# Latent attention on raw latents, the factor per token applied with the takes, rotations between query and key slabs

## The chip, the cores and the metric

The kernel runs on one core of one Trainium2 chip. Its time is device microseconds of one execution. The time before is the median of three runs, 3774.57 us (3770.84 to 3775.61).

## The reference

Two transformer blocks follow each other, both at 512 tokens and width 1024, all in f32. The change touches one mixer of the first block: the latent attention of its second layer. Cut to that part:

```python
def _mla_mixer(u, positions, w_down, q_norm, kv_norm, w_uq, w_ukv, w_out):
    cq, ckv, k_rope = split(u @ w_down, [384, 640])            # 384 + 256 + 64 columns
    q = (_rmsnorm(cq, q_norm) @ w_uq).reshape(b, s, 8, 128 + 64)
    kv = (_rmsnorm(ckv, kv_norm) @ w_ukv).reshape(b, s, 8, 128 + 128)
    q_nope, q_rope = q[..., :128], _rope(q[..., 128:], ...)
    k_nope, v = kv[..., :128], kv[..., 128:]
    k_rope = _rope(k_rope, ...)
    return _mla_attention(q_nope, q_rope, k_nope, k_rope, v) @ w_out
# _rmsnorm(x, g) = x * rsqrt(mean(x * x over the row) + 1e-6) * g
```

The norm of a latent is a gain per column and a factor per token. The gain must come ahead of the projection; the factor is the same for all columns of a token and can be multiplied in before or behind it.

## The kernel before, in words

Activations lie feature by token: `big` has 32 chunks of 128 features by 512 tokens. Weights come in slabs through a ring of four (`ring`), loaded by SyncE in one fixed order (`ORDER`); a slab's load waits until the slab three places ahead has been used up (`lin_done`). A slab of a layer of kind "fm" gives 256 output features for all 512 tokens and fills one of two pairs of PSUM banks (`LP[0]`, `LP[1]`), which alternate by slab. Before TensorE writes a pair again, it waits on `lin_taken0` or `lin_taken1`: VectorE must have copied out the slab before the last. Kind "tm" gives 256 features with the tokens on the partitions. `XB` are four more banks for small products. All engines run one program each, written out in order by hand, and meet only at semaphores; nothing plans or reorders.

Layers marked as cut multiply in three passes with operands split into a high and a low part: ScalarE writes the high part of a slab (`w_hi`, line 1023 by `high`) and GpSimd the rest (`w_lo`, line 1388). The latent attention has these layers:

- `mlad`, 3 slabs, cut: the down projection. Chunks 0 to 2 of `big` (CQ) are the query latent, 3 and 4 (CKV) the key and value latent, 5 (KR) the shared rotary key.
- `mlaq`, 6 slabs, plain f32: queries; chunks 6 to 13 (QN) without, 14 to 17 (QR) with rotation. QR is made by slabs 4 and 5.
- `mlak`, 4 slabs: keys (KN). `mlav`, 4 slabs of kind "tm": values. `mlao`: the output projection behind the attention.

After `mlad` the program before does this (TensorE lines 779 to 787, ScalarE 1247 to 1250, VectorE 1978 to 1988). For each of the two latents ScalarE squares its chunks one by one (`rms`), TensorE sums them over features with a matrix of ones, 512 columns a chunk (`square_sum`), ScalarE takes the root of the 128x512 tile, VectorE its reciprocal (`root`, line 1588) and multiplies chunk by gain and factor (line 1982), in place. `latent_ready` must be 2, both latents done, before TensorE starts `mlaq`. VectorE copies each slab out with one TENSOR_SCALAR of 128x1024 (`plain` line 1745, `tokens` line 1753).

After `mlav` come five rotations (`rotate` on TensorE, `turn` on GpSimd and VectorE): TensorE multiplies a chunk by a rotation matrix, GpSimd multiplies the chunk by the cosines (line 1468), VectorE the rotated one by the sines and adds the two (lines 1761, 1763). Two buffers alternate, so a chunk's rotation waits for the one two ahead. `attention` then waits for all rotations and for all copies (`groups_taken`).

The attention goes over 8 heads by 4 blocks of 128 queries. Unit n: TensorE makes the scores of n (128 to 512 keys wide, lines 449), transposes the probabilities of n - 2 (line 632) and multiplies those of n - 3 with the values. VectorE adds the mask and takes the maximum (line 1786), ScalarE the exponentials (line 1023), VectorE the division (line 1800).

Line 449 is the one matmul helper of the kernel, line 1023 ScalarE's helper. Of an f32 matmul two instructions stand in the trace, so 128x512 by 128x128 is two rows of MATMUL.

Of the kernel before, what the change touches and what calls it, by code (L numbers as in the profile page):

```python
# [23 lines left out]
ALU = mybir.AluOpType  # L24
ACT = mybir.ActivationFunctionType
AX = mybir.AxisListType

P = 128
T = 512
NB = T // P  # L30
# [150 lines left out]
CQ, CKV, KR, QN, QR, KN, MV = 0, 3, 5, 6, 14, 18, 26  # L181
# [4 lines left out]
def build(nc, x, small, consts, consts2, pos, adab, w, out):  # L186
    with ExitStack() as ctx:
        sems = {}

        def s(name):  # L190
            if name not in sems:
                sems[name] = ctx.enter_context(nc.semaphore(name))
            return sems[name]
# [16 lines left out]
        big = sb("big", [P, 32, T])  # L210
        wk = sb("wk", [P, 6, T])
        tabs = sb("tabs", [P, 4, T])
# [13 lines left out]
        rt = sb("rt", [P, T])  # L226
        rstd = sb("rstd", [P, T])
# [46 lines left out]
        def gate_row(i):  # L274

            return big[0:4, (GI, GF, 27, 28, 29)[i], :]

        AD = tmp[:, :, :].rearrange("p a (b t) -> p (a b) t", t=T)
        OD = [tabs[:, 0:3, :].rearrange("p a b -> p (a b)").rearrange("p (j t) -> p j t", j=2),
              wk[:, 0:3, :].rearrange("p a b -> p (a b)").rearrange("p (j t) -> p j t", j=2)]  # L280

        def cc(name, a=0, n=None):
            t, (o, wd) = (cst, COFF[name]) if name in COFF else (cst2, COFF2[name])
            return t[:, o + a:o + (wd if n is None else a + n)]
# [25 lines left out]
        def sp_(name, a=0, n=1):  # L310
            return sm[:, SOFF[name][0] + a:SOFF[name][0] + a + n]

        def blk(b):
            return slice(b * P, (b + 1) * P)
# [130 lines left out]
        def _(pe):  # L445
            pl = Place(pe, s)

            def mm(o, lhsT, rhs, start=True, stop=True):
                return pe.matmul(o, lhsT=lhsT, rhs=rhs, start=start, stop=stop)  # L449
# [79 lines left out]
                pl.ada += n_ada  # L529
                pl.cut += n if cut else 0  # L530

            def square_sum(n, weights):

                if pl.norm:
                    pe.wait_ge(s("rt_ready"), pl.norm)
                for c in range(n):
                    pe.wait_ge(s("sq_ready"), pl.sq + c + 1)
                    mm(XB[0][:, :], weights, sq[:, c % 2, :], start=c == 0, stop=c == n - 1)\
                        .then_inc(s("sq_used"), 1)
                pl.sq += n  # L540
                pl.norm += 1

            def total_sum():

                if pl.norm:
# [52 lines left out]
            def rotate(chunks, weights):  # L598
                for i, c in enumerate(chunks):
                    if pl.rope + i >= 2:  # L600
                        pe.wait_ge(s("rope_done"), pl.rope + i - 1)
                    mm(XB[1 + (pl.rope + i) % 2][:, :], weights, big[:, c, :]).then_inc(s("rot_done"), 1)
                pl.rope += len(chunks)
# [173 lines left out]

            ffn("gu10", "dn10")
            src, fresh = norm(u_hi1)
            linear("mlad", "fm", src, fresh=fresh)  # L780
            square_sum(3, cc("ones"))
            square_sum(2, cc("ones"))
            pl.got("latent_ready", 2)
            linear("mlaq", "fm", lambda c: big[:, CQ + c, :])
            linear("mlak", "fm", lambda c: big[:, CKV + c, :])
            linear("mlav", "tm", lambda c: big[:, CKV + c, :])
            rotate([KR] + list(range(QR, QR + 4)), cc("rot64"))

            def mla_score(hh, _, qb, bank):
                W = (qb + 1) * P  # L790
# [228 lines left out]
        def _(act):  # L1019
            pl = Place(act, s)  # L1020

            def f(o, i, fn, **kw):
                return act.activation(o, i, fn, **kw)  # L1023

            def rms(srcs, size):

                for c, src in enumerate(srcs):
                    if pl.sq + c >= 2:
                        act.wait_ge(s("sq_used"), pl.sq + c - 1)
                    f(sq[:, c % 2, :], src, ACT.Square).then_inc(s("sq_ready"), 1)  # L1030
                pl.sq += len(srcs)
                act.wait_ge(s("sq_used"), pl.sq)
                if pl.norm:
                    act.wait_ge(s("rstd_ready"), pl.norm)
                f(rt[:, :], XB[0][:, :], ACT.Sqrt, scale=1.0 / size, bias=cc("eps")).then_inc(s("rt_ready"), 1)
                pl.norm += 1

            def high(q, it=0):

                slab, width = CUT_SLABS[q]  # L1040
# [6 lines left out]
            def layer(name, take=None, last=False, behind=None):  # L1047


                n = WIDTH[name][0]  # L1050

                def body(k, it):
                    if take:
                        take(k, it)
                    high(pl.cut + k + 2, it)
                    if behind:
                        behind(k)

                slab_loop(act, n - 2, body, peel=n if name in SLAB_ORDER else None)
                for k in (n - 2, n - 1):  # L1060
                    if take:
                        take(k, 0)
                    if not last:
                        high(pl.cut + k + 2)
                    if behind:
                        behind(k)
                pl.slab += n
                pl.group += n
                pl.cut += n
# [174 lines left out]
            hrms()  # L1244
            high(pl.cut + 1)
            high_input(u_hi1, (N_MOD + 3 * 1) * DC)
            layer("mlad", last=True)
            pl.groups_taken()
            rms([big[:, CQ + c, :] for c in range(3)], 384)
            rms([big[:, CKV + c, :] for c in range(2)], 256)  # L1250
            skip("mlaq")
            skip("mlak")
            skip("mlav")
# [270 lines left out]
        def _(dve):  # L1524
# [34 lines left out]
            def take(name, body):  # L1559

                n = WIDTH[name][0]
                n_ada = beside(pl, name)

                def one(k, it):
                    dve.wait_ge(s("lin_done"), at(pl.slab + k + 1, it, RING))
                    body(k, it, (pl.group + k) % 2)
                    if n_ada == n or k < n_ada:
                        ada_take(UP0 + pl.ada + k, it)
                        a = UP0 + 1 + pl.ada + k
                        if a < N_ADA or not isinstance(it, int):  # L1570
                            ada_acc_(a, it)

                slab_loop(dve, n, one, chains=[(link, DC - 1)] if n_ada == n else (),
                          peel=peeled(pl, name, n, n_ada))
                pl.slab += n
                pl.group += n
                pl.ada += n_ada

            def dyn(t, k, it, step, n):

                a = step * k
                return slice(a, a + n) if isinstance(it, int) else bass.ds(it * step * RING + a, n)

            def root():

                dve.wait_ge(s("rt_ready"), pl.norm + 1)
                pl.norm += 1
                dve.reciprocal(rstd[:, :], rt[:, :]).then_inc(s("rstd_ready"), 1)
                dve.wait_ge(s("rstd_ready"), pl.norm)

            def root_total():

# [150 lines left out]
            def plain(dst0):  # L1743
                def body(k, it, p):
                    ts(big[:, bass.ds(it * 2 * RING + 2 * k + dst0, 2) if not isinstance(it, int)
                           else slice(dst0 + 2 * k, dst0 + 2 * k + 2), :], LP[p][:, :, :],
                       1.0, None, ALU.mult)\
                        .then_inc(s(f"lin_taken{p}"), 1)
                return body

            def tokens(dsts):
                def body(k, it, p):
                    ts(dsts[k], LPF[p].rearrange("p (t c) -> p t c", c=256), 1.0, None, ALU.mult)\
                        .then_inc(s(f"lin_taken{p}"), 1)
                return body

            def turn(chunks, t, sines=wk, cosines=S):
                for i, c in enumerate(chunks):
                    k = pl.rope + i
                    dve.wait_ge(s("rot_done"), k + 1)  # L1760
                    link(tt(sines[:, k % 2, :], t, XB[1 + k % 2][:, :], ALU.mult))
                    dve.wait_ge(s("rope_cos"), k + 1)
                    tt(big[:, c, :], sines[:, k % 2, :], cosines[:, k % 2, :], ALU.add).then_inc(s("rope_done"), 1)
                pl.rope += len(chunks)
                dve.wait_ge(s("rope_done"), pl.rope)
# [209 lines left out]

            ffn(1, 0, "gu10", "dn10")
            mod_in(1, 1)
            take("mlad", plain(0))
            for c0, n, name in ((CQ, 3, "q_norm"), (CKV, 2, "kv_norm")):
                root()  # L1980
                for c in range(n):
                    ins = stt(big[:, c0 + c, :], big[:, c0 + c, :], sp_(name, c), rstd[:, :], ALU.mult, ALU.mult)
                ins.then_inc(s("latent_ready"), 1)
                pl.got("latent_ready")
            take("mlaq", plain(QN))
            take("mlak", plain(KN))
            take("mlav", tokens(mv))
            turn([KR] + list(range(QR, QR + 4)), tabs[:, 2, :])
            attention(MLA_H, 192.0 ** -0.5, P, chunked, 0)
            residual(1, 1, "mlao")  # L1990
            ffn(1, 2, "gu11", "dn11")
# [419 lines left out]
```

## Time and profile before

| | |
|---|---|
| median of the runs shown | 3774.57 us |
| profiled execution, its own time | 3773.32 us |
| its span, first to last instruction | 3771.5 us |
| TensorE busy, share of the span | 3607.9 us, 96% |
| VectorE, ScalarE, GpSimd busy | 37%, 26%, 40% |
| mean granted TensorE clock | 0.959 |
| latent attention, end of `mlad` to start of the attention | 1602.3 to 1691.3 us |
| its attention, up to the first matmul of `mlao` | 1691.3 to 1779.7 us |

Times of rows are microseconds from the start of the span. A busy TensorE can be a slow one: its granted clock is either full (1.00, 2.4 GHz) or half (0.50, 1.2 GHz), and a matmul at half level takes up to twice as long while the engine still counts as busy.

### The profile page before, as it was taken

What the parts mean: (1) busy time and instruction counts of PE and PEld (TensorE: products, weight loads), DVE (VectorE), ACT (ScalarE), POOL (GpSimd) and SP (SyncE); (2) the same over time, 40 slices, a digit from 0 to 9 for tenths busy, and PEclk for the clock granted to TensorE, in tenths of its full rate; (3) what the DMA queues carried; (4) which work ended last, traced back from release to release, by engine and by line L of the source; (5) the groups of instructions that cost most, each with busy time, mean ns of one, the idle gap of its engine ahead of it and who ended that gap; (6) DMA issues with size and microseconds to landing.
All of it is one profiled execution on the core that took longest, in us unless ns stands there. A gap on an engine that the chain in (4) does not pass through costs nothing.

```text
span 3771.5 us, 40976 instructions
## 1 busy us (share of the span) xinstructions
PE 3607.9 (96%) x16154; PEld 2739.8 (73%) x16154; DVE 1392.2 (37%) x2572; ACT 966.7 (26%) x1207; POOL 1490.5 (40%) x521
## 2 busy tenths in 40 slices
PE   8999999899999999989999989989999999799999
PEld 7878777468887888745588866843888868437887
DVE  4454277534243422234211135752201167632010
ACT  2222222422223222203222233331212233322221
POOL 3445451035445545400354554401546445014453
PEclk9999998999999999989999989979999999899999
DMA  6434221024343433220223221201222222002222
GB/s 248 186 134 176 98 78 57 1 101 176 131 178 127 177 131 121 76 94 1 76 85 103 89 82 67 79 1 45 78 101 94 85 78 79 12 34 78 99 91 78
DMA packets 53863, 360.57 MB, mean 96 GB/s; under 512 B 5969, under 2 KB 6353, under 8 KB 16593
## 3 DMA queue, kind: packets, MB, share of 16 engines
q1 hardware_dynamic: 53712, 358.53, 26.2%
q8 instruction: 99, 1.62, 0.2%
q14 instruction: 52, 0.42, 0.0%
HBM read 356.41 MB, written 2.10 MB: 95 GB/s over the span
## 4 chain that ended last, share of the span: by engine, by line
PE 90%; DVE 6%; ACT 1%; issue 1%; DMA 1%; POOL 1%; SPq 0%; DVEq 0%; ACTq 0%; POOLq 0%
PE LP L449 80%; PE XB L449 9%; DVE S L1786 1%; PE XB L632 1%; DMA big<-w_ada 1%; PE LP L748 1%; ACT E L1023 0%; DVE tmp L1908 0%; DVE st L1906 0%; ACT sq L1023 0%; POOL wk L1446 0%; DVE gain L1623 0%; DVE wk L1806 0%; POOL w_lo L1388 0%; DVE u L1602 0%
## 5 line engine op out<-in xcount | busy, mean ns | idle before, releaser
L1388 POOL TENSOR_TENSOR w_lo<-ring,w_hi 128x2048 fp32r<-128x2048 f32 (+1 forms) x263 | 1122.8, 4269 | 683.1 <-ACT w_hi L1023 682.3
L449 PE MATMUL LP<-u_hi,w_hi 128*128 128x512 f32 x2480 | 992.0, 400 | 21.2 <-ACT u_hi L1023 17.0
L449 PE MATMUL LP<-u_hi,w_lo 128*128 128x512 f32 x2480 | 979.4, 395 | 0.0
L449 PE MATMUL LP<-u_lo,w_hi 128*128 128x512 f32 x2480 | 937.0, 390 | 0.0
L449 PE MATMUL LP<-big_r,w_hi 128*128 128x512 f32 x2432 | 749.9, 389 | 1.1 <-POOL w_lo L1388 1.1
L1023 ACT ACTIVATE w_hi<-ring 128x2048 fp32r<-128x2048 f32 (+1 forms) x263 | 468.7, 1782 | 823.8 <-PE LP L449 734.0
L449 PEld LDWEIGHTS LP<-u_hi,w_hi 128*128 128x128 f32 x2480 | 474.9, 191 | 136.9 <-issue 39.1
L449 PEld LDWEIGHTS LP<-u_hi,w_lo 128*128 128x128 f32 x2480 | 474.6, 191 | 101.8
L449 PEld LDWEIGHTS LP<-u_lo,w_hi 128*128 128x128 f32 x2480 | 466.4, 188 | 95.2 <-issue 0.5
L449 PEld LDWEIGHTS LP<-big_r,w_hi 128*128 128x128 f32 x2432 | 455.8, 188 | 95.7 <-issue 1.2
L449 PE MATMUL LP<-big_r,w_lo 128*128 128x512 f32 x1216 | 473.2, 389 | 0.0
L1429 POOL TENSOR_TENSOR big_r<-tmp,big_r 128x512 f32 (+2 forms) x120 | 192.4, 1603 | 685.2 <-DVE big_r L1639 685.2
L1446 POOL TENSOR_TENSOR wk<-wk,sq 128x512 f32<-128x512 f32 x66 | 84.7, 1283 | 686.2 <-ACT sq L1023 683.1
L1023 ACT ACTIVATE tmp<-LP 128x512 f32<-128x512 f32 (+1 forms) x120 | 85.5, 712 | 959.7 <-PE LP L449 959.7
L1644 DVE TENSOR_TENSOR tmp<-tmp,LP 128x512 f32<-128x512 f32 x88 | 60.5, 687 | 635.7 <-ACT tmp L1023 620.3
L449 PEld LDWEIGHTS LP<-big_r,w_lo 128*128 128x128 f32 x1216 | 228.2, 188 | 47.6
L449 PE MATMUL LP<-u,ring 128*128 128x512 f32 x512 | 221.9, 594 | 4.2 <-DVE u L2217 2.6
L1545 DVE SCALAR_TENSOR_TENSOR XB<-ada_in,csil,XB 128x256 f32<-128x256 f32 x390 | 191.0, 490 | 13.7
L449 PEld LDWEIGHTS LP<-u,ring 128*128 128x128 f32 x512 | 96.6, 190 | 127.1 <-issue 120.8
L1714 DVE SCALAR_TENSOR_TENSOR h<-LP,gate,h 128x512 f32 (+1 forms) x64 | 48.1, 751 | 356.9 <-PE LP L449 356.4
L1023 ACT ACTIVATE E<-S,stat 128x128 f32<-128x128 f32 (+3 forms) x160 | 89.2, 558 | 265.5 <-DVE stat L1789 188.6
L449 PE MATMUL XB<-big 64*128 64x128 f32 (+5 forms) x472 | 132.1, 515 | 17.2 <-DVE stat L1789 6.1
(260 smaller groups left out, 3193.2 us busy)
## 6 DMA issues: line engine op xcount, KB each, us to landing
ada_in<-w_ada SPq DMA_DIRECT2D x66, 1024.0 KB, 4.9
ring<-w_in SPq DMA_DIRECT2D x22, 1024.0 KB, 4.8
ring<-w_gu00a SPq DMA_DIRECT2D x11, 1024.0 KB, 7.1
ring<-w_gu00b SPq DMA_DIRECT2D x11, 1024.0 KB, 6.7
ring<-w_gu01a SPq DMA_DIRECT2D x11, 1024.0 KB, 6.8
ring<-w_gu01b SPq DMA_DIRECT2D x11, 1024.0 KB, 6.7
ring<-w_gu10a SPq DMA_DIRECT2D x11, 1024.0 KB, 6.7
ring<-w_gu10b SPq DMA_DIRECT2D x11, 1024.0 KB, 6.8
```

The costliest lines, as they stand in the source:

```text
L449: return pe.matmul(o, lhsT=lhsT, rhs=rhs, start=start, stop=stop)
L632: last = pe.transpose(XB[2 + k % 2][:, blk(b)], src[:, blk(b)], cc("ident"))
L748: last = pe.transpose(LP[1][:, j, blk(b)], E[:, 2 * (k % 2) + j, blk(b)], cc("ident"))
L1023: return act.activation(o, i, fn, **kw)
L1388: gp.tensor_tensor(w_lo[:, slab % RING, 0:width], ring[:, slab % RING, 0:width], w_hi[:, q % 2, 0:width].bitcast(F32), ALU.subtract).then_ ...
L1429: gp.tensor_tensor(big_r[:, lo, :], src, big_r[:, hi, :].bitcast(F32), ALU.subtract)\
L1446: gp.tensor_tensor(sqa, sqa, sq[:, c % 2, :], ALU.add).then_inc(s("sq_added"), 1)
L1545: ins = stt(part if c < DC - 1 else ada_acc[:, :], wv[:, c * 256:(c + 1) * 256], csil[:, c:c + 1], part, ALU.mult, ALU.add)
L1644: tt(o, tmp[:, p, 0:T].unsqueeze(1), LP[p][:, 1:2, :], ALU.mult))
L1714: stt(o, LP[p][:, 0:1, :], g, o, ALU.mult, ALU.add).then_inc(s(f"lin_taken{p}"), 1)
L1786: link(dve.tensor_tensor_reduce(out=S[:, k % 2, 0:W], in0=XB[k % 2][:, 0:W], in1=mask(qb, W), scale=1.0, scalar=LOWEST, op0=ALU.add, op1=A ...
```

## The change

`square_sum`, `rms` and `root` go. In their place:

- VectorE takes a slab of `mlad` as two TENSOR_SCALARs of 128x512, each times its gain (`latents`). So `big` holds latents with gain and without the factor per token. Ahead of it ScalarE squares the slab straight from PSUM (`latent_square`); VectorE waits for that.
- The sums over features are made with the tokens on the partitions: the squares are the weights and a single column of ones is moved (`latent_sums`), 12 products for the first latent and 8 for the second. Root and reciprocal are of 128x4. `latent_spread` turns such a column back into a row for all partitions: four products of 128 columns.
- TensorE starts `mlaq` right behind the sums of the first latent. Spread, the second latent's sums, and the rotation of KR stand behind the first three slabs of `mlaq`; the rotations of QR stand behind the first two slabs of `mlak`.
- VectorE copies a slab of `mlaq` or `mlak` out with one TENSOR_TENSOR, times the spread factor; for `mlav` the factor is per partition and block, read with a stride of zero.
- Behind `mlav` nothing is left; the attention waits for the last copy.

```diff
+        RQ, RKV = tabs[:, 0, :], tabs[:, 1, :]
+        def latent_root(i, b=0, n=NB):
+            return st[:, 16 + 4 * i + b:16 + 4 * i + b + n]
+        def latent_squares(c):
+            return Z[:, c, :] if c < 4 else tmpf[:, 1024:1536]
...
-            linear("mlad", "fm", src, fresh=fresh)
-            square_sum(3, cc("ones"))
-            square_sum(2, cc("ones"))
-            pl.got("latent_ready", 2)
-            linear("mlaq", "fm", lambda c: big[:, CQ + c, :])
-            linear("mlak", "fm", lambda c: big[:, CKV + c, :])
+            def latent_sums(i, chunks):
+                pe.wait_ge(s("latent_squared"), i + 2)
+                if i:
+                    pe.wait_ge(s("latent_root"), 1)
+                for c in chunks:
+                    for b in range(NB):
+                        last = mm(XB[3][:, 4 * i + b:4 * i + b + 1], latent_squares(c)[:, blk(b)], cc("ones", 0, 1),
+                                  start=c == chunks[0] and b == 0, stop=c == chunks[-1] and b == NB - 1)
+                last.then_inc(s("latent_summed"), 1)
+            def latent_spread(i):
+                pe.wait_ge(s("latent_recip"), i + 1)
+                if i:
+                    pe.wait_ge(s("latent_copied"), 1)
+                for b in range(NB):
+                    last = mm(XB[0][:, blk(b)], latent_root(i, b, 1).to_broadcast([P, P]), cc("ident"))
+                last.then_inc(s("latent_spread"), 1)
+            def behind_queries(k):
+                if k == 0:
+                    latent_spread(0)
+                    latent_sums(1, range(CKV, CKV + 2))
+                if k == 1:
+                    slab_taken(2)
+                    rotate((KR,), cc("rot64"))
+                if k == 2:
+                    latent_spread(1)
+            def behind_keys(k):
+                if k < 2:
+                    slab_taken(3 + 4 + k)
+                    rotate((QR + 2 * k, QR + 2 * k + 1), cc("rot64"))
+            linear("mlad", "fm", src, fresh=fresh, after=lambda k: latent_sums(0, range(CQ, CQ + 3)) if k == 2 else None)
+            slab_taken(1)
+            linear("mlaq", "fm", lambda c: big[:, CQ + c, :], after=behind_queries)
+            linear("mlak", "fm", lambda c: big[:, CKV + c, :], after=behind_keys)
             linear("mlav", "tm", lambda c: big[:, CKV + c, :])
-            rotate([KR] + list(range(QR, QR + 4)), cc("rot64"))
...
-            rms([big[:, CQ + c, :] for c in range(3)], 384)
-            rms([big[:, CKV + c, :] for c in range(2)], 256)
+            def latent_square(k, it):
+                act.wait_ge(s("lin_done"), pl.slab + k + 1)
...
+                f(o, LP[(first + k) % 2][:, 0:n, :], ACT.Square).then_inc(s("latent_squared"), 1)
+            layer("mlad", latent_square, last=True)
+            for i, size in enumerate((384, 256)):
+                pl.got("latent_summed")
+                f(latent_root(i), XB[3][:, 4 * i:4 * i + NB], ACT.Sqrt, scale=1.0 / size, bias=cc("eps"))\
+                    .then_inc(s("latent_root"), 1)
...
+            def latents(k, it, p):
+                pl.got("latent_squared")
...
+                    ins = ts(big[:, c, :], LP[p][:, i, :], g, None, ALU.mult)
+                ins.then_inc(s(f"lin_taken{p}"), 1)
...
+            def scaled(dst0, tile):
+                def body(k, it, p):
+                    tt(big[:, dst0 + 2 * k:dst0 + 2 * k + 2, :], LP[p][:, :, :],
+                       tile.unsqueeze(1).to_broadcast([P, 2, T]), ALU.mult).then_inc(s(f"lin_taken{p}"), 1)
+                return body
+            def queries_taken(k, it, p):
+                if k == 0:
+                    latent_recip(0)
+                    latent_copy(0, RQ)
+                queries(k, it, p)
+                if k == 0:
+                    latent_recip(1)
+                if k == 1:
+                    turn((KR,), tabs[:, 2, :])
+                if k == 2:
+                    latent_copy(1, RKV)
+            def keys_taken(k, it, p):
+                keys(k, it, p)
+                if k < 2:
+                    turn((QR + 2 * k, QR + 2 * k + 1), tabs[:, 2, :])
```

## Rows read from the trace of the kernel before

**Rows 1.** Chain of waits, 1560 to 1720: start, us, what it went through.
```profile
1567.10 35.16 PE LP L449 x144
...
1608.01 3.36 DVE rstd L1588
...
1618.37 61.05 PE LP L449 x168
1679.41 0.87 PE XB L449 x2
...
1691.33 6.94 PE XB L449 x12
```

**Rows 2.** Busy time by stretch: us, PE, PEld, DVE, ACT, POOL (instructions), clock, DMA, GB/s.
```profile
1560.00:1562.00 2.00, 1.14 (x9) 1.05 (x9) 2.00 (x2) 0.63 (x1) 2.00 (x1) 0.91 0.64 197
1602.00:1612.00 10.00, 5.14 (x12) 1.65 (x10) 5.18 (x3) 4.04 (x7) 0.00 (x0) 1.00 0.13 39
1618.00:1624.00 6.00, 5.63 (x8) 2.57 (x9) 0.31 (x1) 0.00 (x0) 0.00 (x0) 0.58 0.00 0
1679.00:1684.00 5.00, 2.62 (x7) 1.07 (x7) 4.03 (x4) 0.00 (x0) 2.48 (x2) 1.00 0.92 350
1685.00:1711.00 26.00, 23.64 (x51) 11.59 (x52) 9.56 (x34) 5.00 (x16) 3.58 (x3) 0.50 0.07 28
1712.00:1772.00 60.00, 57.80 (x288) 34.61 (x288) 31.29 (x132) 23.16 (x73) 0.00 (x0) 1.00 0.00 1
505.00:560.00 55.00, 55.00 (x228) 40.31 (x227) 44.04 (x51) 11.54 (x14) 28.68 (x11) 1.00 0.22 77
```

**Rows 3.** Timeline, norm ahead of `mlad`: start, us, engine, instruction, [idle before <- releaser].
```profile
1560.97 1.27 PE L449 MATMUL XB<-cst,sq 128*128 128x1 f32 x8 [0.86 <-ACT sq L1023]
...
1563.10 0.18 DVE L1595 RECIPROCAL st<-st 128x4 f32<-128x4 f32 x1
...
1563.34 2.08 PE L449 MATMUL XB<-cst,st 128*128 128x128 f32 x8 [1.09 <-DVE st L1595]
```

**Rows 4.** Groups by line, whole span: count, busy us, mean ns, idle before.
```profile
L1023 ACT ACTIVATE big<-LP 128x1024 f32<-128x1024 f32 x8 | 8.2, 1028 | 39.4 <-PE LP L449 39.4
L2229 DVE TENSOR_TENSOR tmp<-tmp,LP 128x1024 f32<-128x1024 f32 x32 | 39.1, 1221 | 281.1 <-ACT tmp L1023 281.1
```

**Rows 5.** Timeline, slabs of `mlad`, then single products around the two stalls.
```profile
1582.57 4.59 POOL L1388 TENSOR_TENSOR w_lo<-ring,w_hi 128x2048 fp32r<-128x2048 f32 x1 [13.61 <-ACT w_hi L1023]
...
1591.40 1.22 DVE L1745 TENSOR_SCALAR big<-LP 128x1024 f32<-128x1024 f32 x1 [9.66 <-PE LP L449]
...
1604.31 2.94 PE L449 MATMUL XB<-sq,cst 128*128 128x512 f32 x6 [2.07 <-ACT sq L1023]
...
1683.51 1.12 PE L449 MATMUL XB<-big,cst 128*128 128x512 f32 x2 [2.38 <-DVE big L1763]
```

**Rows 6.** Groups by line, 1575 to 1700.
```profile
L1468 POOL TENSOR_TENSOR S<-big,tabs 128x512 f32<-128x512 f32 x5 | 6.3, 1264 | 96.9 <-PE XB L449 94.3 <-DVE big L1763 2.7
...
L1761 DVE TENSOR_TENSOR wk<-tabs,XB 128x512 f32<-128x512 f32 x5 | 3.4, 679 | 0.1
```

**Rows 7.** Timeline of the attention, its first and its last heads.
```profile
1698.47 3.92 PE L449 MATMUL XB<-big 128*128 128x512 f32 x4
...
1713.71 2.08 PE L449 MATMUL XB<-big 128*128 128x512 f32 x4
...
1761.03 0.33 PE L632 MATMUL XB<-cst,E 128*128 128x128 f32 x1
...
1764.60 0.80 PE L449 MATMUL XB<-big 128*128 128x128 f32 x4
...
1766.81 1.22 PE L449 MATMUL XB<-big 128*128 128x256 f32 x4
...
1769.13 1.65 PE L449 MATMUL XB<-big 128*128 128x384 f32 x4
...
1771.77 2.08 PE L449 MATMUL XB<-big 128*128 128x512 f32 x4
```

More of the change, by code:

```diff
@@ L530, in linear @@
                 pl.cut += n if cut else 0
[L532 to L541, printed above, removed]
             def total_sum():
@@ L779, in _, with slab_taken @@
             src, fresh = norm(u_hi1)
-            linear("mlad", "fm", src, fresh=fresh)
-            square_sum(3, cc("ones"))
-            square_sum(2, cc("ones"))
-            pl.got("latent_ready", 2)
-            linear("mlaq", "fm", lambda c: big[:, CQ + c, :])
-            linear("mlak", "fm", lambda c: big[:, CKV + c, :])
+            first = pl.group
+            def slab_taken(k):
+                g = first + k
+                pe.wait_ge(s(f"lin_taken{g % 2}"), g // 2 + 1)
+            def latent_sums(i, chunks):
[31 more added lines that the diff above has]
+            linear("mlak", "fm", lambda c: big[:, CKV + c, :], after=behind_keys)
             linear("mlav", "tm", lambda c: big[:, CKV + c, :])
-            rotate([KR] + list(range(QR, QR + 4)), cc("rot64"))
             def mla_score(hh, _, qb, bank):
@@ L1023, in f @@
                 return act.activation(o, i, fn, **kw)
[L1025 to L1036, printed above, removed]
             def high(q, it=0):
@@ L1246, in _ @@
             high_input(u_hi1, (N_MOD + 3 * 1) * DC)
-            layer("mlad", last=True)
-            pl.groups_taken()
-            rms([big[:, CQ + c, :] for c in range(3)], 384)
-            rms([big[:, CKV + c, :] for c in range(2)], 256)
+            first = pl.group
+            def latent_square(k, it):
+                act.wait_ge(s("lin_done"), pl.slab + k + 1)
+                if k < 2:
+                    o, n = Z[:, 2 * k:2 * k + 2, :], 2
+                else:
+                    o, n = latent_squares(4).unsqueeze(1), 1
+                f(o, LP[(first + k) % 2][:, 0:n, :], ACT.Square).then_inc(s("latent_squared"), 1)
[4 more added lines that the diff above has]
+                    .then_inc(s("latent_root"), 1)
             skip("mlaq")
@@ L1582, in dyn @@
                 return slice(a, a + n) if isinstance(it, int) else bass.ds(it * step * RING + a, n)
[L1584 to L1589, printed above, removed]
             def root_total():
@@ L1977, in _ @@
             mod_in(1, 1)
[L1978 to L1987, printed above, removed]
@@ L1988, in _ @@
-            turn([KR] + list(range(QR, QR + 4)), tabs[:, 2, :])
+            def latents(k, it, p):
+                pl.got("latent_squared")
+                for i, (c, g) in enumerate((((0, sp_("q_norm", 0)), (1, sp_("q_norm", 1))),
+                                            ((2, sp_("q_norm", 2)), (3, sp_("kv_norm", 0))),
+                                            ((4, sp_("kv_norm", 1)), (KR, 1.0)))[k]):
+                    ins = ts(big[:, c, :], LP[p][:, i, :], g, None, ALU.mult)
+                ins.then_inc(s(f"lin_taken{p}"), 1)
@@ new lines, in latent_recip, with latent_copy @@
+            def latent_recip(i):
+                pl.got("latent_root")
+                dve.reciprocal(latent_root(i), latent_root(i)).then_inc(s("latent_recip"), 1)
+            def latent_copy(i, tile):
+                pl.got("latent_spread")
+                dve.tensor_copy(tile, XB[0][:, :]).then_inc(s("latent_copied"), 1)
+                pl.got("latent_copied")
+            def scaled(dst0, tile):
[3 more added lines that the diff above has]
+                return body
@@ new lines, in _ @@
+            queries, keys = scaled(QN, RQ), scaled(KN, RKV)
+            def queries_taken(k, it, p):
[11 more added lines that the diff above has]
+                keys(k, it, p)
+                if k < 2:
+                    turn((QR + 2 * k, QR + 2 * k + 1), tabs[:, 2, :])
@@ L1989, in _, with values_taken @@
+            def values_taken(k, it, p):
+                tt(mv[k], LPF[p].rearrange("p (t c) -> p t c", c=256),
+                   latent_root(1).unsqueeze(2).to_broadcast([P, NB, 256]), ALU.mult).then_inc(s(f"lin_taken{p}"), 1)
+            take("mlad", latents)
+            take("mlaq", queries_taken)
+            take("mlak", keys_taken)
+            take("mlav", values_taken)
             attention(MLA_H, 192.0 ** -0.5, P, chunked, 0)
```

## The prediction

> **What bounds the kernel now.** The page comes first: TensorE is busy 3607.9 of 3771.5 us and fills 90% of the chain that ended last, so time leaves the kernel only where TensorE waits or runs at half clock. Next the chain of waits around the change [rows 1]. `mlad` ends at 1602.26. From there to 1618.37 the chain goes over the last copy, squares, sums, root, a reciprocal of 3.36, multiplies, and for the second latent the same reciprocal and multiplies again: TensorE has nothing large for 16.1 us. Then come 61.05 us of projections, unbroken. From 1679.41 to 1691.33, 11.9 us, the five rotations alternate between TensorE, GpSimd and VectorE. Last the view by stretches, for the clock [rows 2]: 0.58 on the mean of 1618 to 1624, when `mlaq` starts, and 0.50 from 1685 to 1711, through the beginning of the attention, although TensorE was busy 23.64 of those 26 us. From 1712 to 1772 the attention ran at 1.00. So two stalls are to be had, and a slow stretch behind each.
>
> **The stretch from the end of `mlad` to the attention.** Before: 1691.33 - 1602.26 = 89.1 us. After, by TensorE's own order:
>
> - Sums of the first latent: 12 products, 24 instructions of one column. The nearest row is 8 in 1.27 us [rows 3], 0.16 each: 3.8 us. Nothing is waited for: the squares of slabs 0 and 1 are made while slab 2 runs. A square of 128x1024 out of PSUM takes 1.03 us [rows 4]; it now stands ahead of ScalarE's cut of the third slab (and so of GpSimd's rest). That rest ended at 1587.2 and slab 2 began when slab 1 ended, at 1591.4 [rows 5], so 1.03 us is covered; uncovered it would cost that 1.03. VectorE's two smaller copies are about 1.4 us against 1.2 and sit behind the square; the next user of those banks comes a slab later.
> - The projections themselves: 61.05 us, of which a part was at half level: a mean of 0.58 over 6 us is 5.0 us at 0.50, the first 0.4 of them before the start, so about 4.7 us that held 2.4 us of work [rows 1, 2]. At full level 58.7 us. SyncE's loads keep their order and waits; each slab now takes as long or longer, so they only gain room.
> - Behind slab 0 of `mlaq`: VectorE's reciprocal of 128x4 is queued behind its wait for that slab, so TensorE waits for it. 0.18 us and two handoffs (from 1563.10 to 1563.34 for the like [rows 3]): 0.4 us with the end of the slab.
> - Two spreads: 8 instructions in 2.08 us at half level [rows 3]. Between 1.0 (if all of it scales) and 2.1 each; I take 1.1, as weights of 128 columns must be loaded too. 2.2 us for both.
> - Sums of the second latent: 16 instructions, 2.5 us.
> - Five rotations at 0.87 [rows 1]: 4.3 us. What GpSimd and VectorE do for them (1.26 us and twice about 0.7 [rows 6]) lies beside the next slabs. The tightest place is the second pair of QR: it needs the first pair's additions, some 4.4 us after they began, and TensorE has 1.7 us of rotation and a slab of `mlak` (8 instructions of 0.43) ahead of it, 5.1 us. Cost 0; if that cover fails it costs the difference, below 1 us. The rotations of the hybrid layer stand between slabs in the same way, in a stretch where TensorE was busy 55 of 55 us at 1.00 [rows 2].
> - Takes by TENSOR_TENSOR: 1.22 us for 128x1024 with one operand in PSUM [rows 4], and 1.22 for the copy now [rows 5]. Cost 0. The one with a stride of zero has no row; between 1.2 and, say, twice that; a slab of `mlav` is 3.4 us, so it hides, save the last.
> - End: the attention now waits for the last copy, 1.2 us and a handoff, 1.4 us. The rotations hid that before.
>
> Sum: 3.8 + 58.7 + 0.4 + 2.2 + 2.5 + 4.3 + 1.4 = 73.3 us. That is 15.8 less than 89.1.
>
> **The attention behind it.** No instruction of it changes, only the clock it starts at. The fourth unit's scores begin at 1698.47, those of the next head at 1713.71, 15.24 us later; from there to 1771.77 six heads take 9.68 us each [rows 7]. The first head thus lost 15.24 - 9.68 = 5.6 us. Its ramp, 1691.33 to 1698.47, was 7.14 us; three score groups at full level are 0.80 + 1.22 + 1.65 and a transpose of 0.33 [rows 7], 4.0 us: 3.1 us more. Worth 8.7 us if the clock stays up. TensorE's gap ahead of it is now 1.4 us. Where the clock held at 1.00 through waits (1602 to 1612, 5.14 us busy of 10) there had been a gap of 2.1 us; where it fell, between 1684 and 1685, one of 2.4 us [rows 2, 5]. I expect it to hold. From 0 to 8.7.
>
> **The clock inside the new stretch.** This is the added cost I am least sure of. With instructions of one column the engine is busy but works little. Ahead of `mlad` 16 such, with a gap of 0.9 us, ended in a fall of the clock (0.91 in 1560 to 1562) [rows 2, 3]. Now 24 follow `mlad` and about 4 us of spread and sums stand behind slab 0. Each may bring a spell like that at 1618, which cost 2.4 us [rows 2]. Between 0 and 2 x 3.4; I take one spell, 2.5 us. The Trainium skill (TensorE: Matmul & The Clock Gate, section "Why this matters for your kernels") blames gaps in which the engine is idle for drops in mid-kernel. The sums are no such gap, so by it no spell would come and the gain would be 24.5 us; the fall in rows 2 began right after one-column work, which is why my term stays.
>
> Total: 15.8 + 8.7 - 2.5 = 22.0 us. The profiled execution (3773.32 us; 1.8 around its span) would become 3751.3. It was 1.25 us below the median shown, so against that median: 3774.57 - 22.0 = 3752.6 us.
>
> **Rivals.**
>
> 1. *The attention still starts at half clock.* The gap of 1.4 us together with the narrow first units is enough for a fall, and once down the narrow units did not bring it up for 20 us in the trace of before. The 8.7 us stay lost: gain 13.3, 3761.3 us. For it speaks the long 0.50 row; against it the ten microseconds at 1.00 with half the time idle. The Trainium skill (TensorE: Matmul & The Clock Gate, Part 4: PE-mode transpose) says that transposes don't count as busy for the clock as other matmuls do; by it this rival is likelier, yet 60 us of attention with transposes in every unit ran at 1.00 [rows 2], so it alone does not bring the clock down.
> 2. *The new handoffs bind.* VectorE now has reciprocal, two copies and three turns in its queue between takes, and each take holds a PSUM pair. If takes come late, TensorE waits at up to six slabs, about 1 us each, and with one longer spell (3.4 instead of 2.5) the gain is 15 us: 3759.6. Against it: VectorE's work per slab of `mlak` is 1.2 + 2 x 1.6, under the 5.1 us from slab to slab.
> 3. *Slower: the interleaved products hold the clock down.* If every small group throws TensorE to half level and the short slabs between don't bring it back, each microsecond spent at half level loses half of itself. It decides at 49 us at half level in a stretch of some 90: then the 24.5 us are gone. With all of the 73 us and the attention's start at half: 3774.6 - 15.8 + 73 = about 3832. Against it stands the hybrid layer's stretch, 55 us with rotations between slabs at 1.00 [rows 2].
> 4. *It changes nothing*, since the norm was hidden. The chain shows it was not [rows 1].
>
> **How the numbers follow.** Forecast 0.70, with its own range 3748 to 3758 (0 to 2 spells, and the executions before lie 5 us apart); rival 1 0.17; rival 2 0.09; rival 3 0.02; rival 4 0.02. The range to 3764 takes in rivals 1 and 2. 0.2%, 7.5 us, is what a measurement of this kernel can tell from none: all but rivals 3, 4 and the tail of 2 are beyond it. Faster 0.94, within 0.2% 0.04, slower 0.02.
>
> **What would show it.** In the new profile: from the last matmul of `mlad` to the first of `mlaq` about 4 us, all of it one-column products; `mlaq` to the end of `mlav` without a TensorE wait over 1 us; 1.4 us to the first scores; 0.50 for no more than 5 us or so in all before the attention and 1.00 in its first head, whose spacing is 9.7 instead of 15.2 us. Wrong if the first scores come more than 76 us after `mlad` (rivals 2 or 3), or if the first head shows 0.50 (rival 1), or if time comes back behind the attention.

## The result, and the profile after

The changed kernel takes 3747.72 us, median of four runs (3746.4 to 3749.99), against 3772.7 us before (four runs, 3768.0 to 3775.61). The ratio is 0.9931, 95% interval 0.9919 to 0.9944: 26 us faster, between 21 and 31. The four runs of before are the three shown ahead and one more at 3768.0 us, so this median of before is 1.9 us lower than the 3774.57 us from which the prediction counted. The profiled execution took 3749.99 us, its span is 3748.2 us.

The chain of waits of the changed kernel over the stretch that the prediction worked out (start, us, what):

```profile
1605.98 2.57 PE XB L459 x24
1608.55 5.27 PE LP L459 x12
1613.83 0.02 issue
1613.85 0.19 DVE st L2016
1614.04 0.04 issue
1614.08 2.84 PE XB L459 x24
1616.92 6.95 PE LP L459 x12
1623.88 0.86 PE XB L459 x2
1624.73 5.15 PE LP L459 x12
1629.88 0.89 PE XB L459 x8
1630.78 18.89 PE LP L459 x44
1649.66 1.72 PE XB L459 x4
1651.38 3.43 PE LP L459 x8
1654.81 1.72 PE XB L459 x4
1656.53 20.69 PE LP L459 x80
1677.22 0.02 issue
1677.24 1.24 DVE tmp L2049
1678.48 0.04 issue
1678.53 3.84 PE XB L459 x12
```

`mlad` ends at 1605.98. From there the chain is TensorE's but for two places: the reciprocal at 1613.85, with a wait of 0.25 us, and the last copy of `mlav` at 1677.24, 1.3 us. Both 3.36 us reciprocals of [rows 1] are gone, and so is the alternation of the rotations. The one slab that stands out is the second of `mlaq`, 6.95 us where its neighbours take 5.15. The view by stretches shows why (us, PE, PEld, DVE, ACT, POOL, clock, DMA, GB/s); these lines answer to [rows 2]:

```profile
1608.00:1614.00 6.00, 5.81 (x17) 2.59 (x17) 0.22 (x2) 0.26 (x1) 0.00 (x0) 1.00 0.04 17
1616.00:1620.00 4.00, 4.00 (x13) 2.23 (x13) 1.40 (x2) 1.55 (x2) 0.00 (x0) 0.61 0.09 29
1620.00:1676.00 56.00, 56.00 (x167) 30.76 (x166) 23.68 (x23) 0.00 (x0) 6.25 (x5) 1.00 0.28 87
1676.00:1700.00 24.00, 21.95 (x101) 12.48 (x99) 12.05 (x50) 8.69 (x28) 0.00 (x0) 1.00 0.32 133
```

In the third column from the end of a row, the granted clock, a mean of 0.61 over 4 us is about 3 us at half level, the kind of spell that the prediction speaks of. From the end of `mlad` to the end of the attention the clock falls nowhere else. In the kernel before, it was at 0.50 for the first 21 us of the attention. The first heads of the changed kernel's attention in the timeline of TensorE, which answer to [rows 7]:

```profile
1682.46 2.08 PE L459 MATMUL XB<-big 128*128 128x512 f32 x4
...
1692.14 2.08 PE L459 MATMUL XB<-big 128*128 128x512 f32 x4
```

9.68 us from head to head, where the first took 15.24.

For what follows the time is cut at three points that every trace shows: the last matmul of `mlad`, the first scores, and the first matmul of `mlao`. The rest, from there to the end of the span, is the same program in every kernel of this study, some 2000 us of it. All numbers are us of one profiled execution; "attention" runs from the first scores to the first matmul of `mlao`.

| kernel | mlad to scores | attention | both | rest |
|---|---|---|---|---|
| before | 89.1 | 88.4 | 177.5 | 1991.8 |
| changed | 72.5 | 79.7 | 152.2 | 1990.0 |
| changed, second profile | 72.5 | 79.7 | 152.2 | 2000.7 |
| rotations put back | 78.7 | 85.3 | 164.0 | 1991.9 |
| rotations alone | 82.8 | 79.6 | 162.4 | 1996.9 |
| before, with fillers | 90.1 | 79.6 | 169.7 | 2000.0 |
| wide sums | 70.8 | 79.7 | 150.5 | 2002.2 |
| wide sums, second profile | 70.8 | 79.7 | 150.5 | 1991.5 |
| early scores | 71.2 | 79.4 | 150.6 | 2002.0 |
| all three edits | 69.0 | 79.4 | 148.4 | 1990.2 |

So the change itself is worth 177.5 - 152.2 = 25.3 us, and the last column, which no edit touches, moves by 12. The stages ahead vary too: `mlad` ended between 1596.7 us (with fillers) and 1606.0 us (changed).

### The profile page after: what moved, and what is told of

Its sections match the earlier page's. It is cut to its first block, busy times and chain, and to the rows that moved or that the text cites. A ratio compares the mean times of both kernels' runs of the same rounds, so it can differ in the third digit from the quotient of the medians.

```text
span 3748.2 us, 41071 instructions
## 1 busy us (share of the span) xinstructions
PE 3597.0 (96%) x16200; PEld 2740.0 (73%) x16200; DVE 1385.3 (37%) x2572; ACT 965.4 (26%) x1205; POOL 1490.6 (40%) x521
## 4 chain that ended last, share of the span: by engine, by line
PE 90%; DVE 6%; ACT 1%; issue 1%; DMA 1%; POOL 1%; SPq 0%; DVEq 0%; ACTq 0%; POOLq 0%
PE LP L459 80%; PE XB L459 9%; DVE S L1814 1%; PE LP L747 1%; DMA big<-w_ada 1%; PE XB L631 0%; ACT E L1060 0%; DVE tmp L1936 0%; DVE st L1934 0%; POOL wk L1481 0%; ACT sq L1060 0%; DVE wk L1834 0%; DVE gain L1651 0%; DVE stat L1826 0%; POOL w_lo L1423 0%
## 5 line engine op out<-in xcount | busy, mean ns | idle before, releaser
L2296 DVE TENSOR_TENSOR tmp<-tmp,LP 128x1024 f32<-128x1024 f32 x32 | 39.1, 1222 | 280.9 <-ACT tmp L1060 280.9
```

Of the source, the lines that this page charges most:

```text
L2296: cut_hidden(k, it, p, pl.low, 2, lambda o: tt(o, o, LP[p][:, :, :], ALU.mult))
```

## Experiments

**Rotations put back.** The changed kernel, the rotations behind `mlav` again; `turn`, their part on GpSimd and VectorE, moves back with them (not shown):

```diff
-                if k == 1:
-                    slab_taken(2)
-                    rotate((KR,), cc("rot64"))
...
-            linear("mlak", "fm", lambda c: big[:, CKV + c, :], after=behind_keys)
+            linear("mlak", "fm", lambda c: big[:, CKV + c, :])
             linear("mlav", "tm", lambda c: big[:, CKV + c, :])
+            rotate([KR] + list(range(QR, QR + 4)), cc("rot64"))
```

> The changed kernel with the five rotations put back behind mlav, all else of the change kept. Theory (two separate gains, and the rotations' stall also costs the clock of the attention): the stretch from the end of mlad to the first scores grows by 6.3 us (11.9 us of alternating rotations against 4.3 us of rotations between slabs and a last wait of 1.3), and the first head of the attention runs at half level again, 8.7 us. So 10 us are left of the gain: a ratio of 0.9973 to the kernel before. Rival (most of the gain is the norm's, the rotations were a small matter): the gain stays above 17 us, ratio under 0.9955. Rival (the half level of the attention came from the norm's stall and its late recovery): the first head shows 1.00 and 19 us are left.

Measured: 3761.4 us (six runs), ratio 0.9973 (0.9961 to 0.9985), to the digit what the first theory gave, but in part by luck. By the stretches, 6.2 of the expected 6.3 us came back ahead of the scores, and only 5.6 of the expected 8.7 in the attention, so that 13.5 us of the gain are left in place and not 10. The first lines of its attention (timeline of TensorE), and the clock in it:

```profile
1681.22 6.61 PE L459 MATMUL XB<-big 128*128 128x128 f32 x12 [2.52 <-DVE big L1784]
...
1688.02 3.92 PE L459 MATMUL XB<-big 128*128 128x512 f32 x4
...
1700.43 2.08 PE L459 MATMUL XB<-big 128*128 128x512 f32 x4
```

```profile
1682.50:1695.00 12.50, 12.50 (x26) 5.59 (x27) 4.64 (x23) 3.35 (x11) 0.00 (x0) 0.50 0.00 1
1696.00:1760.00 64.00, 61.79 (x306) 36.76 (x305) 32.91 (x137) 24.75 (x78) 0.00 (x0) 1.00 0.00 1
```

The same code at the same place started slow again, 6.61 us for the first three units against 3.84, but the first head took 12.41 us, not 15.24: the clock came back about 14 us after the first scores instead of 21. How long it stays down is not the same in the two kernels, though the attention is the same. Both rivals fall: the gain by the ratio is not above 17 us, and the first head does show 0.50.

**Rotations alone.** The kernel before, and only its rotations moved between the slabs. `behind_queries` and `behind_keys` are those of the change with the rotations alone, and `turn` moves along (both not shown):

```diff
-            linear("mlaq", "fm", lambda c: big[:, CQ + c, :])
-            linear("mlak", "fm", lambda c: big[:, CKV + c, :])
+            linear("mlaq", "fm", lambda c: big[:, CQ + c, :], after=behind_queries)
+            linear("mlak", "fm", lambda c: big[:, CKV + c, :], after=behind_keys)
             linear("mlav", "tm", lambda c: big[:, CKV + c, :])
-            rotate([KR] + list(range(QR, QR + 4)), cc("rot64"))
```

> The kernel before with the rotations alone moved between the query and key slabs; norms, sums and plain copies as they were. Theory: TensorE's stall of 16.1 us behind mlad and the half level at the start of mlaq stay; the stretch to the first scores shrinks by 6.3 us and the attention starts at full level, 8.7 us, its first head 9.7 us instead of 15.2: ratio 0.9960. With the run above it adds up to the whole, about 25 us. Rival (the parts overlap and each alone gets less, as a stall filled in one place comes back in the other): the two sum to under 18 us.

Measured: 3762.84 us (six runs), ratio 0.9968 (0.9956 to 0.998). Its chain of waits:

```profile
1618.16 12.89 PE LP L449 x24
1631.05 0.86 PE XB L449 x2
1631.91 24.03 PE LP L449 x56
...
1662.81 20.69 PE LP L449 x80
...
1683.52 1.24 DVE tmp L1768
...
1684.81 3.84 PE XB L449 x12
```

6.3 us off the first stretch and 8.8 off the attention, where 6.3 and 8.7 were expected; the expected ratio of 0.9960 lies within the interval. `mlaq` still starts late and slow (24 instructions in 12.89 us). Together the two halves, 13.5 and 15.1 us by the stretches, make 3.3 us more than the whole 25.3. The experiment before accounts for it: its attention lost 5.6 us to the clock and not 8.7. The rival, that the halves take from each other and sum to under 18 us, falls.

**Before, with fillers.** The stall stays; TensorE gets seven products more.

```diff
+                    for _ in range(fill[i] if fill else 0):
+                        mm(XB[0][:, :], weights, cc("chunk"))
...
-            rotate([KR] + list(range(QR, QR + 4)), cc("rot64"))
+            rotate([KR] + list(range(QR, QR + 4)), cc("rot64"), (0, 2, 0, 1, 4))
```

> The kernel before with its stall of rotations left where it is; only TensorE gets seven extra products of 128x512 whose result nobody reads, in the gaps between the rotations (two behind the second, one behind the fourth, four behind the last). It does more work, not less. Theory (8.7 us of the gain are the clock's alone): the clock holds at 1.00 through the rotations and the first head, spacing 9.7 us; the fillers delay the chain by 1 us at most: ratio 0.9980, a gain of 7 to 8.7 us. Rival (the first head is slow for its own order, waits between engines, and not for the clock): no gain, ratio 1.000 or above, spacing of the first head above 13 us.

TensorE's timeline of it, and the clock:

```profile
1675.43 1.88 PE L449 MATMUL XB<-cst 128*128 128x512 f32 x4
1677.98 1.12 PE L449 MATMUL XB<-big,cst 128*128 128x512 f32 x2 [0.67 <-DVE big L1765]
...
1683.41 3.60 PE L449 MATMUL XB<-cst 128*128 128x512 f32 x8
1686.84 3.74 PE L449 MATMUL XB<-big 128*128 128x128 f32 x12
...
1690.67 2.08 PE L449 MATMUL XB<-big 128*128 128x512 f32 x4
...
1700.35 2.08 PE L449 MATMUL XB<-big 128*128 128x512 f32 x4
```

```profile
1680.00:1760.00 80.00, 76.27 (x353) 43.35 (x351) 42.09 (x165) 28.55 (x91) 3.06 (x3) 1.00 0.02 7
```

Where there was a gap of 2.38 us [rows 5] there is one of 0.67, the first three units take 3.74 instead of 6.94 us, the first head 9.68 instead of 15.24, and the clock is at 1.00 throughout. The first stretch is 1.0 us longer for the fillers, the attention 8.8 us shorter, by useless work alone. No instruction of the attention differs, so the 8.8 us are the clock's, and the rival, waits of the first head's own order, falls. In the total the expectation, a ratio of 0.9980, missed: 3770.77 us (11 runs), ratio 0.9992 (0.9983 to 1.0001). That is a gain of 3 us, at most 6.4, not clear of none, where 7.8 were won in place. The profiled execution has a rest 8.2 us longer than the one of before, 2000.0 against 1991.8, and stages ahead of the end of `mlad` that are 5.5 us shorter. Whether long rests are commoner with the fillers is not known.

**Wide sums.** The same number of products, with 128 columns of ones moved instead of one (ScalarE then reads one column of each 128 for its root, not shown):

```diff
-                        last = mm(XB[3][:, 4 * i + b:4 * i + b + 1], latent_squares(c)[:, blk(b)], cc("ones", 0, 1),
+                        last = mm(XB[3][:, blk(b)], latent_squares(c)[:, blk(b)], cc("ones"),
```

> The changed kernel with the sums of squares made by 128 columns of ones instead of one column: same count of instructions, same weights, 128 times the columns. Theory (a one-column product takes as long as its weight load, 0.107 us, and does almost no work for the clock): the sums take 2.6 us as before, the stretch of 3.4 us at half level behind slab 0 of mlaq goes, and from the end of mlad to the first scores it is 70.8 instead of 72.6 us. Rival (the fall comes from the wait and the spread, not from the narrow products): the spell stays. In the total 1.8 us can't be told from none; the view by stretches decides.

Its chain from the end of `mlad`, and the clock:

```profile
1601.89 2.68 PE XB L459 x24
1604.57 5.17 PE LP L459 x12
...
1610.00 2.94 PE XB L459 x24
1612.94 5.15 PE LP L459 x12
```

```profile
1610.00:1618.00 8.00, 8.00 (x37) 5.13 (x38) 2.09 (x3) 1.55 (x2) 0.00 (x0) 1.00 0.18 51
```

The sums take 2.68 instead of 2.57 us, the second slab 5.15 instead of 6.95 at a clock of 1.00, the stretch 70.8 us: the first theory, to the tenth. The wait and the spread are still there, so they alone do not bring the fall. But its two runs were 3756.35 and 3754.07 us, ratio 0.995 (0.9932 to 0.9968), no better than the changed kernel for 1.7 us won. Was that the edit or chance? The next two runs ask.

**The changed kernel and the wide sums, each a second time.**

> The changed kernel once more, unaltered, for a second profile. Theory A (the spell at half level behind slab 0 of mlaq and the lengths of the spells in the stages behind the attention, 1990 to 2002 us so far for the same instructions, differ from execution to execution by where the clock's falls happen to lie): stretch from mlad to the first scores 71 to 76 us, attention 79.7 us, but the rest behind it not the 1990.0 us of the first profile. Theory B (they are fixed by the program): the second profile repeats 72.6, 79.7 and 1990.0 within 1 us.

> The variant with sums by 128 columns of ones once more, unaltered. If the narrow products cause the spell behind slab 0 of mlaq, it is absent here a second time and the stretch is 70.8 us again. If it was luck, it may show, with 72 to 75 us. For the total: theory A of the run above has its median within 3 us of the changed kernel's, 3747 to 3752 us, with the first two runs (3754 and 3756) the high end of a spread; theory B, that wide columns cost something later on, keeps it at 3755.

The changed kernel: 3748.97 us (five runs, 3747.44 to 3758.39), ratio 0.9938 (0.9925 to 0.9951). Its profiled execution was the one at 3758.39, with the very same 72.5 and 79.7 us, and a rest of 2000.7 us instead of 1990.0. So for the rest theory A holds, that it differs from execution to execution, and theory B falls by 10.7 us. But the spell behind slab 0 of `mlaq`, which theory A counted among the things that differ, came back the same. The same 220 us of the rest, from 600 us behind the first matmul of `mlao`, first profile and second:

```profile
2358.18:2578.18 220.00, 198.16 (x1028) 118.68 (x1027) 128.19 (x274) 70.18 (x138) 30.61 (x15) 0.88 0.07 25
```

```profile
2355.88:2575.88 220.00, 200.90 (x1015) 118.63 (x1015) 126.95 (x273) 70.13 (x138) 30.61 (x15) 0.84 0.07 25
```

One program, one stretch, 0.88 and 0.84: 220 x 0.04 = 9 us of full clock less, most of the 10.7 us. By position it comes out the same: a slab of 24 matmuls that the first execution starts 789.5 us behind the first matmul of `mlao` starts 798.4 us behind it in the second. In the four traces with a rest of 2000 us or more it starts at 797.7 to 799.8, in the other six at 789.3 to 795.2.

The wide sums went the other way: the second profile has 70.8 us again and a rest of 1991.5, its execution 3746.39 us; the four runs beside it were 3754.11 to 3760.12, median of five 3755.72, ratio 0.9957 (0.9945 to 0.997). That median is above what theory A allowed (3747 to 3752) and is what theory B gave for it (3755), but theory B's reason, a cost of wide columns later on, does not fit the rest of 1991.5. So long and short rests occur with either kernel, but not equally often: six of seven runs of the wide sums took 3754 us or more, and one of nine of the changed kernel. Whether an edit ahead of them shifts the odds is open.

For the spell ahead of the attention the traces agree. It stood in each of the four traces of the changed kernel and its variants with one-column sums, and in none of the three with wide ones. In three of the four it followed the second sums, behind slab 0 of `mlaq`; in the early-scores kernel below it followed the first sums, and slab 0 took 6.97 us.

**Early scores.** The attention's wait for the last copy goes behind the first three units:

```diff
-                pl.groups_taken()
+                if not early:
+                    pl.groups_taken()
...
                     if n >= 3:
+                        if early and n == 3:
+                            pl.groups_taken()
```

> The changed kernel, with the attention's wait for the last copy of mlav moved from ahead of the first scores to ahead of the first product with the values, three units later. Theory (TensorE's 1.3 us gap behind mlav is pure waiting, the scores need nothing of mlav): from the end of mlav to the fourth unit's scores 4.2 instead of 5.4 us; VectorE's first maximum still queues behind its last copy, which leaves it a small wait. Rival (the wait only moves to the first maximum): 5.4 us again. In the total it can't be seen.

```profile
1664.75 6.85 PE L459 MATMUL LP<-ring,big 128*128 128x256 f32 x31
1671.44 3.74 PE L459 MATMUL XB<-big 128*128 128x128 f32 x12
...
1675.27 2.08 PE L459 MATMUL XB<-big 128*128 128x512 f32 x4
```

The first scores follow `mlav` without a gap, and the fourth unit's come 3.8 us after its end; by the chain of the changed kernel they came 5.4 us after it (1677.22 to 1682.62). 1.6 us won, where 1.2 was expected. The total, 3754.76 us (four runs), ratio 0.9951 (0.9937 to 0.9966), is above the changed kernel's 3748.97 all the same; its profiled execution again carries a long rest, 2002.0.

**All three edits.** Wide sums, early scores, and VectorE's first reciprocal ahead of its wait for slab 0:

```diff
             take("mlad", latents)
+            latent_recip(0)
...
             def queries_taken(k, it, p):
                 if k == 0:
-                    latent_recip(0)
```

> The changed kernel with three edits: sums by 128 columns, the first reciprocal ahead of VectorE's wait for slab 0 of mlaq (TensorE then has no wait of 0.3 us there), and the early first scores. If each does what the view by stretches says: 1.8 + 0.3 + 1.2 us off the 152.2 us from the end of mlad to the first matmul of mlao, 149 us. Against the changed kernel's median of 3747.7 that is 3744 to 3745 us, less than the spread of its runs, so the total may not show it. Rival: an early reciprocal costs VectorE time ahead of slab 0's take and nothing is won.

```profile
1600.19 2.68 PE XB L459 x24
1602.87 5.15 PE LP L459 x12
1608.02 2.68 PE XB L459 x24
1610.70 5.15 PE LP L459 x12
```

TensorE no longer waits from `mlad` to the attention. Both stretches together take 148.4 us, 3.8 less than in the changed kernel, where 3.3 were expected. Its six runs fall into two groups: 3739.1 and 3740.54, the lowest of the study, and 3751.38 to 3752.59. Median 3751.69, ratio 0.9938 (0.9926 to 0.9951), the same as the changed kernel's in that series. In place it beats the changed kernel; in the median it is not shown to.

## Why the prediction came out as it did

The mechanism was right, step by step. What failed is the size of terms in the sum for the stretch from `mlad` to the scores, the one-column sums first, and with them a range too narrow on its low side. The gain was forecast at 22.0 us and measured at 25.3 in place.

- *One-column sums, the term that was mis-sized most.* The prediction took 0.16 us an instruction from a row of 8 in 1.27 us [rows 3], which makes 3.8 + 2.5 = 6.3 us for 40. The first 24 took 2.57 us, 0.107 each, and the other 16 about 1.7, together some 4.3: 2 us less. The row was no fair price. The granted clock falls to 0.50 inside it, at about 1561.7, and a row of the timeline runs to the end of its last instruction: the same 24 are 2.73 us there and 2.57 in the chain. In the changed kernel's trace rows of 8 take 0.95 to 1.05 us. The Trainium skill (TensorE: Matmul & The Clock Gate, section "LDWEIGHTS (loading the stationary operand)") gives a weight load as columns divided by 1.2 GHz, by which an estimate for 128 columns is 0.107 us; the pace of 2.57 / 24 agrees with it. That the load sets the pace is not shown by itself, but 128 moving columns in place of one only raise it to 0.112 us.
- *The other terms of that stretch.* Forecast 73.3 us and 2.5 for the clock, 75.8; measured 72.5. Of the 3.3 us missed, the sums and the two spreads make 2.2 (3.8 against 2.57; the first spread with the second sums 3.6 against 2.84; the second spread 1.1 against 0.89), the clock 0.7, and the projections, the wait and the last copy 0.1 or so each.
- *The clock in that stretch.* Forecast one spell and 2.5 us. One came, behind slab 0, and cost 6.95 - 5.15 = 1.8 us. The cause named, narrow products, is borne out by the wide sums. By the rule cited in the prediction from the Trainium skill (TensorE: Matmul & The Clock Gate, section "Why this matters for your kernels"), that idle gaps cause such falls, none would have come; here the engine was at work up to a wait of 0.25 us, and it fell. The 3.4 us that bound the term from above in the prediction have no row behind them as a cost.
- *Wait behind slab 0, rotations, last copy.* 0.4, 4.3 and 1.4 us forecast; 0.25, 4.3 and 1.3 measured. VectorE's copies out of PSUM with a second operand cost nothing more than plain ones: 1.225 us each, with a stride of zero 1.224. The square ahead of ScalarE's cut was covered; slab 2 of `mlad` did not wait.
- *The attention.* Forecast 8.7 us if the clock held, its likeliest case; measured 8.8 (88.4 to 79.7 us, rounded). Ramp and first head came as forecast, 3.9 us and 9.68. The fillers show it as the clock's.
- *Rivals.* The first (attention at half clock), the third and the fourth did not happen. Of the second nothing is seen: no slab of `mlaq` or `mlak` but the one with the spell is longer than 5.27 us.
- *The total.* The median, 3747.72 us, lies 0.3 us below the range's low end of 3748; the ratio times the 3772.7 us of before gives 3746.7. With the 3.3 us of mis-sized terms put right, the forecast of 3752.6 would have been 3749.3. The remaining 1.6 us to the median have no step of the sum behind them: the profiled executions differ by 23.3 us and not by 25.3, since `mlad` ended 3.7 us later than before and the rest was 1.8 us shorter, and neither of these is the change's work. The range took the runs' 5 us as noise about one value, while the rest alone moves between 1990 and 2002 us from trace to trace. That the median came to lie just outside and not just inside was a matter of which executions were measured.

## What to carry to other kernels

Where an engine's chain of small steps stands between two stages of matmuls, count it twice: once as the wait, and again for the clock at which the next stage may start; here the 11.9 us of rotations cost 6.3 us in place and 8.8 us in the attention behind it. A factor that is the same for all columns can go behind the product, into a copy that has to be made anyway; here that cost nothing, 1.225 us against 1.22. And when an edit is worth a few microseconds, measure it between fixed points of the trace and not by the total.

## What the runs showed of the hardware

- One-column products run at 0.107 us each, 128-column ones at 0.112 (2.68 for 24), yet a fall of the granted clock to 0.50 followed them only in the four traces with the former, and in none of the three with the latter.
- The clock's spells are not always the same from one execution of a program to the next: 0.88 and 0.84 over the same 220 us, 10.7 us in the whole rest. The runs of the last kernel fall into two groups, 3739 to 3741 and 3751 to 3753 us; no trace of the second group was taken, so that the rest makes them is not shown.
- An attention that starts at half level can stay there: for 21 us in the kernel before and about 14 with the rotations put back. Where it started at 1.00 it held that, 80 us with the fillers.
- Useless work can shorten a stage: seven products of 128x512 more, 7.8 us less from the end of `mlad` to `mlao`. The whole kernel was not shown to gain by it.
